# Meta rows as the fixed side of the first stage's products, and the recurrence's factors made in that stage

## The chip, the cores and the metric

The kernel runs on one core of one Trainium2 chip. The metric is the device time of one launch in microseconds (us); less is better.

## What is computed

Two transformer-like blocks run one after the other on 512 tokens of width 1024. The change touches only the first part of the first block:

```python
h = concat([zeros(112 rows), meta_tokens (16 rows), x (512 rows)])
a = rmsnorm(h, g_mix)
proj = einsum('bld,de->ble', a, w_in)                 # w_in: 1024 x 3584
sb_q, sb_k, sb_v, hg_q, hg_f, hg_i, hg_g = split(proj) # seven groups of 512 columns

o_sb = stick_breaking_attention(sb_q, sb_k, sb_v)      # 8 heads of 64
log_f = log(lb + (1 - lb) * sigmoid(hg_f))             # forget factors
k_in  = where(real, (1 - lb) * sigmoid(-hg_f), 0)      # keys
q_in  = silu(hg_q)
o_hg = hgrn2_chunked(q_in, k_in, hg_i, log_f) * silu(hg_g)   # 4 heads of 128
```

The 16 meta rows are needed only as keys and values of later rows, so their projection is made only for the groups k, v, f (`hf`) and i (`hi`). Then follow an output product, 32 experts of which each token uses two, and a second block with a convolution, a state-space branch and a feed-forward part. None of these is changed.

## The kernel before

The kernel is written instruction by instruction for each engine. TensorE (PE) multiplies, ScalarE (ACT) and VectorE (DVE) copy and combine, GpSimd (POOL) does a little elementwise work, SyncE (SP) starts the loads. Each engine has one queue in the order of its code; `wait_ge` on a semaphore orders them. The function `stage_a` holds three stages with a barrier after each (`g["clear"]`): the first stage (projections), the attention stage, and the recurrence stage.

A weight matrix is used in two halves of precision. ACT copies a loaded unit to `whi` (rounded to the product's format), DVE subtracts it from the original to get `wlo`. The normed input is kept in the same two halves, turned, as `aT_hi` and `aT_lo`. Each product is then three: low with high, high with low, and high with high.

The first stage walks over 14 units (numbered 0 to 13) of 2048 weights per partition, two for each of the groups q, k, v, hq, hf, hi, hg. For each, SP loads the unit, ACT makes `whi` (`make_hi`, line 245), DVE makes `wlo` (`make_lo`, line 320), and PE multiplies. There are two kinds of unit:

- Turned groups (q, k, hq, hf): a unit holds 256 columns in 8 pieces of depth. The weights are the fixed side (the one loaded into the array), the 512 tokens move past: lines 432, 437, 438. For k and hf the 16 meta rows move past the same weights in three products of 16 columns, lines 434 to 436.
- Plain groups (v, hi, hg): a unit holds 512 columns in 4 pieces of depth. The tokens are the fixed side in tiles of 128, the weights move past (`split_mm`, lines 48 to 50). `tiles_of` adds a fifth tile for the meta rows in v and hi; it is 128 rows wide, of which 16 are meta rows and the rest zeros.

`wused` counts units that PE has finished with. `make_hi(u)` waits for it, so that buffer u % 2 is free. ACT empties the results (`evacuate`); for k and hf it also empties the 16 meta columns of each of four column blocks.

Three things that the recurrence stage reads are made in the attention stage, between the attention's own instructions: ACT turns the sigmoids in `hfT` into forget factors (`forget`, line 621, one of four heads after each of pieces 2 to 5), DVE scales `sgn` into keys (`keys`, line 732), and POOL multiplies `q1` (line 680) and then seven levels of decays (line 686), each from neighbouring pairs of the level before.

The attention stage has 24 pieces, three for each of 8 heads. For each piece PE makes scores (lines 525 and 530), ACT takes their absolute value, exponential and logarithm (lines 599 to 603), DVE forms the sums and splits them in two halves (lines 703 to 714: the cast at 712 makes `qh`, the subtraction at 714 makes `ql`), PE sums tails over `ql` and `qh` (lines 538 to 543), ACT exponentiates (line 618). PE multiplies a head's weights with the values in `values` (line 562), once for each head, 10 products which the trace counts as 20.

## Time and profile before

| | |
|---|---|
| median of 3 runs (lowest to highest) | 2279.46 us (2278.56 to 2281.94) |
| profiled execution, its own time | 2279.0 us |
| its span, first to last instruction | 2276.8 us |
| mean granted TensorE clock | 0.940 of full speed |
| busy: PE, PE weight load, DVE, ACT, POOL | 90%, 72%, 60%, 47%, 8% |
| first stage's products, by the trace | 20.74 to 210.31 us |
| attention stage, by the trace | 210.31 to 311.66 us |

Busy shares are means over stages with different limits. The length of a matmul in the trace goes from its start to the end of its passage through the array, and the next one starts before that; how fast PE works is read from start to start. The granted clock is a share of 2.4 GHz; in a short stretch it is 1.00 (2.4 GHz), 0.50 (1.2 GHz) or a mean of the two.

### The profile page before, as it was taken

What the parts mean: (1) busy time and instruction counts of PE and PEld (TensorE: products, weight loads), DVE (VectorE), ACT (ScalarE), POOL (GpSimd) and SP (SyncE); (2) the same over time, 40 slices, a digit from 0 to 9 for tenths busy, and PEclk for the clock granted to TensorE, in tenths of its full rate; (3) what the DMA queues carried; (4) which work ended last, traced back from release to release, by engine and by line L of the source; (5) the groups of instructions that cost most, each with busy time, mean ns of one, the idle gap of its engine ahead of it and who ended that gap; (6) DMA issues with size and microseconds to landing.
All of it is one profiled execution on the core that took longest, in us unless ns stands there. A gap on an engine that the chain in (4) does not pass through costs nothing. (4 is left out here: it accounts for less than half of the span.)

```text
span 2276.8 us, 25098 instructions
## 1 busy us (share of the span) xinstructions
PE 2054.9 (90%) x10173; PEld 1636.9 (72%) x10173; DVE 1361.3 (60%) x1510; ACT 1066.6 (47%) x1252; POOL 173.3 (8%) x130
## 2 busy tenths in 40 slices
PE   7999988699999999938799999988698988999997
PEld 6887677566666666627688888877487766888786
DVE  4112775588998898842398888877533254333223
ACT  4223623388888888832334445545242233223112
POOL 1000100012222222200000000000000000000000
PEclk9999899899999999976899999999899998999999
DMA  5120004389999999851333333322222213333221
GB/s 181 61 69 1 1 1 160 114 337 403 406 402 406 400 402 395 343 178 41 94 93 93 93 93 93 93 74 56 74 78 89 92 56 85 107 95 93 92 93 56
DMA packets 201776, 346.84 MB, mean 152 GB/s; under 512 B 13587, under 2 KB 149259, under 8 KB 184251
## 3 DMA queue, kind: packets, MB, share of 16 engines
q1 hardware_dynamic: 194171, 333.42, 41.9%
q0 software_dynamic: 5120, 8.40, 1.1%
q10 hardware_dynamic: 2368, 3.39, 0.5%
q8 instruction: 82, 1.34, 0.2%
q14 instruction: 35, 0.29, 0.0%
HBM read 340.91 MB, written 12.65 MB: 155 GB/s over the span
## 5 line engine op out<-in xcount | busy, mean ns | idle before, releaser
L1492 DVE TENSOR_TENSOR wlo_e<-raw_e,whi_e 128x2048 fp32r<-128x2048 f32 x190 | 431.7, 2288 | 56.6 <-ACT whi_e L1417 56.1
L1789 DVE TENSOR_TENSOR w_lo<-w_raw,w_hi 128x2048 fp32r<-128x2048 f32 x89 | 203.8, 2289 | 322.2 <-ACT w_hi L1781 322.2
L1417 ACT CAST whi_e<-raw_e 128x2048 fp32r<-128x2048 f32 x188 | 359.2, 1912 | 74.6 <-PE pall L1568 40.7
L1781 ACT CAST w_hi<-w_raw 128x2048 fp32r<-128x2048 f32 x89 | 169.4, 1904 | 429.5 <-PE pall L50 415.1
L48 PE MATMUL pall<-hT_hi,w_lo 128*128 128x512 f32 x864 | 348.1, 403 | 23.1 <-DVE xbc L2333 10.3
L49 PE MATMUL pall<-hT_lo,w_hi 128*128 128x512 f32 x864 | 342.3, 396 | 0.0
L50 PE MATMUL pall<-hT_hi,w_hi 128*128 128x512 f32 x864 | 341.8, 396 | 0.0
L1567 PE MATMUL pall<-whi_e,xs 128*128 128x512 f32 x512 | 210.0, 410 | 4.2 <-DVE xs L1497 4.2
L48 PEld LDWEIGHTS pall<-hT_hi,w_lo 128*128 128x128 f32 x864 | 166.4, 193 | 59.7 <-DVE xbc L2333 10.5
L1568 PE MATMUL pall<-wlo_e,xs 128*64 128x512 f32 x512 | 206.3, 403 | 0.0
L50 PEld LDWEIGHTS pall<-hT_hi,w_hi 128*128 128x128 f32 x864 | 165.8, 192 | 35.5
L49 PEld LDWEIGHTS pall<-hT_lo,w_hi 128*128 128x128 f32 x864 | 166.2, 192 | 35.0 <-issue 0.5
L1567 PEld LDWEIGHTS pall<-whi_e,xs 128*128 128x128 f32 x512 | 99.4, 194 | 55.9 <-DVE xs L1497 5.4
L2318 DVE SCALAR_TENSOR_TENSOR mixed<-yT,cols,mixed 128x512 f32<-128x512 f32 x180 | 126.3, 747 | 0.0
L48 PE MATMUL pall<-w_hi,hT_lo 128*128 128x256 f32 (+1 forms) x320 | 98.9, 309 | 9.5 <-DVE hT_lo L2779 9.1
L48 PE MATMUL pall<-whi_e,hT_lo 128*64 128x512 f32 x256 | 100.6, 393 | 4.0 <-issue 2.4
L50 PE MATMUL pall<-whi_e,hT_hi 128*64 128x512 f32 x256 | 100.6, 393 | 0.0
L49 PE MATMUL pall<-wlo_e,hT_hi 128*64 128x512 f32 x256 | 100.4, 392 | 0.0
L2936 DVE TENSOR_TENSOR mixed<-mixed,pall 128x512 f32<-128x512 f32 x22 | 15.1, 688 | 139.5 <-PE pall L50 139.5
L50 PE MATMUL pall<-w_hi,hT_hi 128*128 128x256 f32 (+1 forms) x320 | 97.9, 306 | 0.0
L49 PE MATMUL pall<-w_lo,hT_hi 128*128 128x256 f32 (+1 forms) x320 | 97.8, 306 | 0.0
L971 POOL DMA_INDIRECT xg<-m_rows,row_x x32 | 81.8, 2557 | 67.4 <-PE pall L1558 36.2
(468 smaller groups left out, 3788.7 us busy)
## 6 DMA issues: line engine op xcount, KB each, us to landing
raw_e<-in_w_expert_up_dram SPq DMA_DIRECT2D x64, 1024.0 KB, 11.2
raw_e<-in_w_expert_down_dram SPq DMA_DIRECT2D x64, 1024.0 KB, 11.8
raw_e<-in_w_expert_gate_dram SPq DMA_DIRECT2D x64, 1024.0 KB, 11.7
w_raw<-in_w_in_dram SPq DMA_DIRECT2D x80, 512.0 KB, 6.2
w_raw<-in_w_gate_up_dram SPq DMA_DIRECT2D x44, 512.0 KB, 5.1
w_raw<-in_w_down_dram SPq DMA_DIRECT2D x22, 512.0 KB, 4.1
mixed<-in_w_in_dram SPq DMA_DIRECT2D x10, 1024.0 KB, 5.0
A<-acs_rows SPq DMA_DIRECT2D x8, 1024.0 KB, 4.9
```

The source lines that it names most:

```text
L48: nc.tensor.matmul(out, w_lo, m_hi, start=start, stop=False)
L49: nc.tensor.matmul(out, w_hi, m_lo, start=False, stop=False)
L50: return nc.tensor.matmul(out, w_hi, m_hi, start=False, stop=stop)
L971: pool.indirect_dma_start(xg[0:SLOTS, :], None, m_rows, bass.IndirectOffsetOnAxis(g["row_x"][0:SLOTS, b:b + 1], 0), bounds_check=T - 1, oo ...
L1417: nc.scalar.copy(whi[j], raw[j]).then_inc(sem_hi, 1)
L1492: nc.vector.tensor_tensor(wlo[j], raw[j], whi[j].bitcast(F32), ALU.subtract).then_inc(sem_lo, 1)
L1567: mm(out, x[:, kk, :], k4(whi[j])[:, k, :], start=kk == 0, stop=False, skip_group_check=True)
L1568: last = mm(out[0:SLOTS, :], x[:, kk, 0:SLOTS], k4(wlo[j])[:, k, :], start=False, stop=kk == KD - 1, skip_group_check=True)
L1781: self.nc.scalar.copy(self.hi[i][:, :], self.raw[i][:, :]).then_inc(self.s_hi, 1)
L1789: (engine or self.nc.vector).tensor_tensor(self.lo[i][:, :], self.raw[i][:, :], self.hi[i][:, :].bitcast(F32), ALU.subtract).then_inc(self ...
L2318: ins = V.scalar_tensor_tensor(mixT[:, c, :], src, col("dw_w_a", k * KD + c), mixT[:, c, :], ALU.mult, ALU.add)
L2936: V.tensor_tensor(hd, sg, banks[(2 * c + 1) % 8], ALU.mult).then_inc(s["hd"], 1)
```

## The change

The meta rows get a store of their own, `mT`, with 8 pieces of depth, each of 32 columns: 16 of the high half, 16 of the low half. The padding tile in `aT_hi` and `aT_lo` goes. In each unit of k, v, hf and hi, after the tokens' products, a new `meta_part` runs with the meta rows as the fixed side and the weights moving past: per piece of depth one product of the 32 columns with `whi`, and one of the 16 high columns with `wlo`. In k and hf the weights move in 256 columns, in v and hi in 512. After the second unit of a group ACT copies the 32 x 512 result out (`meta_sums`), and a small product with a selecting matrix `sel` adds rows 0 to 15 to rows 16 to 31 (`meta_turn`); for k and hf it also turns the result. `meta_turn` and the copy `meta_out` stand in the first unit of the next group.

`forget`, `keys`, `q1` and the decays move from the attention stage into the first. Some buffers share memory with others to make room, and a clearing of the meta buffer at the start is gone.

```diff
@@ tiles
             def tiles_of(what):
-                return [0, 1, 2, 3] if what == "hg" else [0, 1, 2, 3, 4]
+                return [0, 1, 2, 3]
@@ gpsimd, first stage (the same lines are taken out of the attention stage)
+                pool.wait_ge(s["mask"], 1)
+                pool.wait_ge(s["f"], HG_HEADS)
+                nc.gpsimd.tensor_tensor(q1[:, :, :], hqT[:, :, :], hfT[:, :, META:TM], ALU.mult).then_inc(s["q1"], 1)
+                for i, w in enumerate(WIDE):
+                    if i >= 1:
+                        pool.wait_ge(s["dec"], i)
+                    of = decay[w // 2][:, :, 1:1 + T // 16] if w == 32 else decay[w // 2][:, :, :]
+                    pairs = of.rearrange("p e (n two) -> p e n two", two=2)
+                    nc.gpsimd.tensor_tensor(decay[w][:, :, :], pairs[:, :, :, 0], pairs[:, :, :, 1], ALU.mult).then_inc(s["dec"], 1)
@@ scalar, first stage
+                def meta_sums(m, u):
+                    act.wait_ge(s["wused"], u + 1)
+                    if m >= 1:
+                        act.wait_ge(s["mt"], m)
+                    nc.scalar.copy(msb[:, :], MB[0:2 * META, :]).then_inc(s["ms"], 1)
+
+                def meta_out(what):
+                    act.wait_ge(s["mt"], META_OF[what] + 1)
...
+                    if half == 0 and u >= 1 and units[u - 1][1] in META_OF:
+                        if u + 2 < len(units):
+                            make_hi(u + 2)
+                        meta_out(units[u - 1][1])
+                        if units[u - 1][1] == "hf":
+                            act.wait_ge(s["evac"], o)
+                            act.wait_ge(s["mev"], META_OF["hf"] + 1)
+                            for e in range(HG_HEADS):
+                                forget(e)
+                        continue
+                    if half and what in META_OF:
+                        meta_sums(META_OF[what], u)
@@ vector, first stage
                 for u in range(2, len(units)):
                     make_lo(u)
+                dve.wait_ge(s["mev"], META_OF["hf"] + 1)
+                dve.wait_ge(s["evac"], 20)
+                dve.wait_ge(s["lb"], 2)
+                for e in range(HG_HEADS):
+                    keys(e)
@@ tensor, first stage
+                def meta_part(what, half, wh, wl):
+                    if half == 0 and META_OF[what] >= 1:
+                        pe.wait_ge(s["ms"], META_OF[what])
+                    wide = wh.shape[-1]
+                    c = slice(half * wide, half * wide + wide) if wide == 256 else slice(0, wide)
+                    for k in range(wh.shape[1]):
+                        kk = k if wide == 256 else 4 * half + k
+                        st, sp_ = (k == 0, k == KD - 1) if wide == 256 else (kk == 0, kk == KD - 1)
+                        nc.tensor.matmul(MB[0:2 * META, c], mT[:, kk, :], wh[:, k, :], start=st, stop=False, skip_group_check=True)
+                        last = nc.tensor.matmul(MB[0:META, c], mT[:, kk, 0:META], wl[:, k, :], start=False, stop=sp_,
+                                                skip_group_check=True)
+                    return last
+
+                def meta_turn(what):
+                    m = META_OF[what]
+                    pe.wait_ge(s["ms"], m + 1)
+                    pe.wait_ge(s["sel"], 1)
+                    if m >= 1:
+                        pe.wait_ge(s["mev"], m)
+                    if what in ("k", "hf"):
+                        for e in range(4):
+                            last = nc.tensor.matmul(MT[:, e * META:e * META + META], msb[:, e * P:e * P + P], sel[:, :], start=True,
+                                                    stop=True)
+                    else:
+                        last = nc.tensor.matmul(MT[0:META, :], sel[:, :], msb[:, :], start=True, stop=True)
+                    last.then_inc(s["mt"], 1)
...
                                 nc.tensor.matmul(b[:, :], w_l, a_hi, start=st, stop=False)
-                                if is_meta_turned(what):
-                                    nc.tensor.matmul(bm[:, 0:META], w_l, m_hi, start=st, stop=False)
-                                    nc.tensor.matmul(bm[:, 0:META], w_h, m_lo, start=False, stop=False)
-                                    nc.tensor.matmul(bm[:, 0:META], w_h, m_hi, start=False, stop=sp_)
                                 nc.tensor.matmul(b[:, :], w_h, a_lo, start=False, stop=False)
...
+                    if half == 0 and u >= 1 and units[u - 1][1] in META_OF:
+                        meta_turn(units[u - 1][1])
+                    if what in META_OF:
+                        meta_part(what, half, wh, wl).then_inc(s["wused"], 1)
@@ attention stage
-                    if 2 <= n < 2 + HG_HEADS:
-                        forget(n - 2)
...
-                    if 6 <= n < 6 + HG_HEADS:
-                        keys(n - 6)
```

How the instructions move is shown at three places. First PE's queue in a unit of k, over one piece of depth. Before, with the three products of 16 columns (the last size in a row is that of the result):

```order
L432 MATMUL pall<-aT_hi,wlo_a 128x512
L434 MATMUL pall<-aT_hi,wlo_a 128x16
L435 MATMUL pall<-aT_lo,whi_a 128x16
L436 MATMUL pall<-aT_hi,whi_a 128x16
L437 MATMUL pall<-aT_lo,whi_a 128x512
L438 MATMUL pall<-aT_hi,whi_a 128x512
```

After, at the end of the same unit, where the tokens' products are followed by those of the meta rows (`mT_a` is `mT`), eight pairs in all:

```order
L533 MATMUL pall<-aT_hi,wlo_a 128x512
L534 MATMUL pall<-aT_lo,whi_a 128x512
L535 MATMUL pall<-aT_hi,whi_a 128x512
L490 MATMUL pall<-whi_a,mT_a 32x256
L491 MATMUL pall<-wlo_a,mT_a 16x256
L490 MATMUL pall<-whi_a,mT_a 32x256
L491 MATMUL pall<-wlo_a,mT_a 16x256
```

The narrow products no longer stand between wide ones. Second, PE's queue in the first unit of v, after the last tokens' products; the first row is `meta_turn` for k, the rest are the meta rows of v:

```order
L503 MATMUL pall<-sel,meta_rows 128x16 x4
L490 MATMUL pall<-whi_a,mT_a 32x512
L491 MATMUL pall<-wlo_a,mT_a 16x512
L490 MATMUL pall<-whi_a,mT_a 32x512
L491 MATMUL pall<-wlo_a,mT_a 16x512
```

They stand where the fifth tile of lines 48 to 50 stood. Third, POOL's queue. Before, `q1` (called `q` here) and the decays come last in the attention stage:

```order
L677 AFFINE_SELECT own_rows<-own_rows 128x8
L680 TENSOR_TENSOR q<-hqT,hfT 128x2048
L686 TENSOR_TENSOR decay<-hfT 128x1056
L686 TENSOR_TENSOR decay<-decay 128x528
L686 TENSOR_TENSOR decay<-decay 128x264
```

After, they follow POOL's only large instruction of the first stage, ahead of the barrier:

```order
L229 TENSOR_TENSOR wlo_a<-mixed,whi_a 128x2048
L232 TENSOR_TENSOR q<-hqT,hfT 128x2048
L238 TENSOR_TENSOR decay<-hfT 128x1056
L238 TENSOR_TENSOR decay_rest<-decay 128x528
L238 TENSOR_TENSOR decay_rest<-decay_rest 128x264
```

On ACT the four `forget` instructions now stand in unit 10, between the cast for unit 12 and the copies of unit 11's results:

```order
L266 CAST whi_a<-mixed 128x2048
L334 ACTIVATE hfT<-pall 128x4x16
L335 ACTIVATE sgn<-pall 128x4x16
L341 ACTIVATE hfT<-hfT,lb,omlb 128x528 x4
L317 COPY hv_nat<-pall 128x512 x4
L326 COPY meta_rows<-pall 32x512
L266 CAST whi_a<-mixed 128x2048
```

In the attention stage they stood singly behind pieces 2 to 5.

## Rows read from the trace of the kernel before

**Rows 1.** Windows over two stages: length, busy time and instructions by engine, clock, DMA.

```profile
20.74:210.31 189.57, 189.53 (x924) 159.19 (x924) 36.00 (x34) 50.38 (x71) 0.00 (x0) 0.99 0.19 62
210.31:311.66 101.35, 90.78 (x381) 61.09 (x381) 70.65 (x135) 61.76 (x118) 13.01 (x21) 0.85 0.00 1
```

**Rows 2.** Timeline of PE in the first stage: start, length, line, operation.

```profile
45.36 0.39 PE L432 MATMUL pall<-aT_hi,wlo_a 128*128 128x512 f32 x1
...
46.04 0.39 PE L432 MATMUL pall<-aT_hi,wlo_a 128*128 128x512 f32 x1
...
62.55 0.40 PE L432 MATMUL pall<-aT_hi,wlo_a 128*128 128x512 f32 x1
```

**Rows 3.** Timeline of PE in the attention stage.

```profile
225.29 1.12 PE L580 MATMUL pall<-v_nat,pick_m 16*128 16x512 f32 x2
...
232.75 2.39 PE L562 MATMUL pall<-v_nat,ww 128*128 128x64 f32 x20
...
241.33 2.40 PE L562 MATMUL pall<-v_nat,ww 128*128 128x64 f32 x20
...
253.95 4.47 PE L562 MATMUL pall<-v_nat,ww 128*128 128x64 f32 x20
...
268.77 2.39 PE L562 MATMUL pall<-v_nat,ww 128*128 128x64 f32 x20
...
277.36 2.39 PE L562 MATMUL pall<-v_nat,ww 128*128 128x64 f32 x20
```

**Rows 4.** Timeline of POOL in the attention stage.

```profile
242.03 4.54 POOL L680 TENSOR_TENSOR q<-hqT,hfT 128x2048 f32<-128x2048 f32 x1 [27.36 <-ACT hfT L621]
...
248.73 3.83 POOL L686 TENSOR_TENSOR decay<-decay 128x528 f32<-128x528 f32 x6
```

**Rows 5.** Timeline of DVE in the attention stage.

```profile
233.01 0.43 DVE L712 CAST qh<-qq 128x512 fp32r<-128x512 f32 x1
...
242.10 4.75 DVE L712 CAST qh<-qq 128x512 fp32r<-128x512 f32 x1
246.89 2.31 DVE L714 TENSOR_TENSOR ql<-qq,qh 128x512 fp32r<-128x512 f32 x1
```

**Rows 6.** Windows of 3.4 us in the attention stage.

```profile
247.60:251.00 3.40, 1.74 (x7) 1.31 (x7) 3.23 (x4) 1.64 (x3) 3.17 (x4) 0.92 0.00 0
251.00:254.40 3.40, 3.40 (x12) 2.74 (x11) 3.26 (x9) 2.11 (x5) 1.33 (x4) 0.50 0.03 7
...
268.00:271.40 3.40, 3.40 (x28) 3.10 (x27) 2.09 (x5) 1.92 (x4) 0.00 (x0) 1.00 0.00 0
```

**Rows 7.** Timeline of ACT in the first stage, late units.

```profile
177.67 0.59 ACT L294 COPY hv_nat<-pall 128x512 f32<-128x512 f32 x1 [0.76 <-PE pall L50]
...
188.55 0.59 ACT L294 COPY hv_nat<-pall 128x512 f32<-128x512 f32 x1 [2.13 <-PE pall L50]
189.03 1.91 ACT L245 CAST whi_a<-mixed 128x2048 fp32r<-128x2048 f32 x1
...
202.15 0.60 ACT L296 ACTIVATE hg_nat<-pall 128x512 f32<-128x512 f32 x1 [9.91 <-PE pall L50]
```

**Rows 8.** Timeline of PE far behind, products of 256 columns.

```profile
1299.77 0.28 PE L49 MATMUL pall<-w_lo,hT_hi 128*128 128x256 f32 x1
...
1303.97 0.28 PE L48 MATMUL pall<-w_hi,hT_lo 128*128 128x256 f32 x1
```

**Rows 9.** Timeline of PE, where products of 128 and 64 output columns meet.

```profile
802.70 0.40 PE L1568 MATMUL pall<-wlo_e,xs 128*64 128x512 f32 x1
802.98 0.41 PE L48 MATMUL pall<-whi_e,hT_lo 128*64 128x512 f32 x1
803.24 0.39 PE L49 MATMUL pall<-wlo_e,hT_hi 128*64 128x512 f32 x1
```

**Rows 10.** Timeline of DVE in the first stage, late.

```profile
190.97 2.29 DVE L320 TENSOR_TENSOR wlo_a<-mixed,whi_a 128x2048 fp32r<-128x2048 f32 x1 [11.74 <-ACT whi_a L245]
```

**Rows 11.** Timeline of ACT in the attention stage, one step of forget().

```profile
241.13 0.81 ACT L621 ACTIVATE hfT<-hfT,lb,omlb 128x528 f32<-128x528 f32 x1
```

More of the change, by code:

```diff
@@ L93, in stage_a @@
         ident_r = sb("ident_r", [P, P], F32R)
+        q1 = sb("q1", [P, HG_HEADS, T])
+        WIDE = (2, 4, 8, 16, 32, 64, 128)
+        sizes = [TM // w if w <= META else T // w for w in WIDE]
+        decay2 = sb("decay2", [P, HG_HEADS, sizes[0]])
+        decay_rest = sb("decay_rest", [P, HG_HEADS * sum(sizes[1:])])
+        decay, at = {1: hfT, 2: decay2}, 0
+        for w, n in zip(WIDE[1:], sizes[1:]):
+            decay[w] = decay_rest[:, at:at + HG_HEADS * n].rearrange("p (e n) -> p e n", e=HG_HEADS)
+            at += HG_HEADS * n
         s = {n: sem("a_" + n) for n in (
-            "x meta vec gbc ident ones eps hm0 ssq rt rs xn tr hi lo vtr cols lbd lb whi wlo wused out evac "
-            "it xor xf up ge mask never wlo0".split())}
+            "x meta vec gbc ident ones eps ssq rt rs xn tr hi lo vtr cols lbd lb whi wlo wused out evac "
+            "it xor xf up ge mask never wlo0 sel ms mt mev f kx q1 dec".split())}
         s_x = [sem(f"a_x{i}") for i in range(NT)]
@@ L143, in stage_a @@
                     outs.append((what, e))
-            def is_meta_turned(what):
-                return what in ("k", "hf")
+            META_OF = {"k": 0, "v": 1, "hf": 2, "hi": 3}
+            MB, MT = banks[6], banks[7]
             def turn_bank(j):
@@ L245, in make_hi, with upper_meta @@
                     nc.scalar.copy(whi[u % 2][:, :], raw[u % 3]).then_inc(s["whi"], 1)
+                def upper_meta():
+                    act.wait_ge(s["tr"], 2 * NT + 1)
+                    nc.scalar.copy(mT[:, :, 0:META], banks[6][:, 0:KD * META].rearrange("p (k t) -> p k t", k=KD)).then_inc(s["hi"], 1)
                 def upper(j):
@@ L282, in evacuate @@
                     elif what == "k":
-                        nc.scalar.copy(kT[:, e, META:TM], b[:, :])
-                        last = nc.scalar.copy(kT[:, e, 0:META], banks[6 + e % 2][:, 0:META])
+                        last = nc.scalar.copy(kT[:, e, META:TM], b[:, :])
                     elif what == "hf":
                         for dst, sign in ((hfT, 1.0), (sgn, -1.0)):
-                            nc.scalar.activation(dst[:, e, META:TM], b[:, :], ACT.Sigmoid, scale=sign)
-                            last = nc.scalar.activation(dst[:, e, 0:META], banks[6 + e % 2][:, 0:META], ACT.Sigmoid, scale=sign)
+                            last = nc.scalar.activation(dst[:, e, META:TM], b[:, :], ACT.Sigmoid, scale=sign)
                     elif what == "v":
@@ L297, in evacuate, with forget @@
                     last.then_inc(s["evac"], 1)
+                def meta_sums(m, u):
[5 more added lines that the diff above has]
+                    act.wait_ge(s["mt"], META_OF[what] + 1)
+                    by_e = MT[:, 0:4 * META].rearrange("p (e t) -> p e t", e=4)
+                    if what == "k":
+                        last = nc.scalar.copy(kT[:, :, 0:META], by_e)
+                    elif what == "hf":
+                        nc.scalar.activation(hfT[:, :, 0:META], by_e, ACT.Sigmoid)
+                        last = nc.scalar.activation(sgn[:, :, 0:META], by_e, ACT.Sigmoid, scale=-1.0)
+                    else:
+                        last = nc.scalar.copy((v_nat if what == "v" else hv_nat)[0:META, NT, :], MT[0:META, :])
+                    last.then_inc(s["mev"], 1)
+                def forget(e):
+                    nc.scalar.activation(hfT[:, e, :], hfT[:, e, :], ACT.Identity, bias=lb[:, e:e + 1],
+                                         scale=omlb[:, e:e + 1]).then_inc(s["f"], 1)
                 o = 0
@@ L352, in _ @@
                 make_lo(1)
-                lower(4)
+                lower_meta()
+                nc.vector.tensor_tensor(sel[:, :], ident[0:2 * META, 0:META], ident[0:2 * META, META:2 * META],
+                                        ALU.add).then_inc(s["sel"], 1)
                 dve.wait_ge(s["vtr"], 1)
@@ L402, in turn, with turn_meta @@
                         last.then_inc(s["tr"], 1)
+                def turn_meta():
+                    pe.wait_ge(s["xn"], NT + 1)
+                    for k in range(KD):
+                        last = nc.tensor.transpose(banks[6][:, k * META:k * META + META], xn[NT % 2][0:META, k * P:k * P + P],
+                                                   ident[0:META, 0:META])
+                    last.then_inc(s["tr"], 1)
+                def meta_part(what, half, wh, wl):
[20 more added lines that the diff above has]
+                                                    stop=True)
+                    else:
+                        last = nc.tensor.matmul(MT[0:META, :], sel[:, :], msb[:, :], start=True, stop=True)
+                    last.then_inc(s["mt"], 1)
                 for j in range(NT):
@@ L409, in _ @@
                     if u == 1:
-                        turn(NT)
+                        turn_meta()
                         vectors()
@@ L452, in _ @@
                             if j == tiles_of(what)[-1]:
-                                last.then_inc(s["wused"], 1)
+                                if what not in META_OF:
+                                    last.then_inc(s["wused"], 1)
                             elif half:
```

69 lines of the change are left out of this document (28 added, 41 removed).

## The prediction

> **What bounds the kernel now.** I read the windows by stage first, then PE's timeline in the first stage, then PE, POOL and DVE side by side in the attention stage.
>
> In the first stage PE is the bound: in 189.57 us of products it is busy 189.53 us at a granted clock of 0.99, DVE works 36.0 us and ACT 50.4 us [rows 1]. What PE no longer does there comes off the time, one for one, as long as the halves `whi` and `wlo` come in time. The reader is to see that a product of 512 columns costs 0.227 us from start to start (0.68 us for the three of a piece of depth) [rows 2].
>
> In the attention stage the pace is read from one `values` to the next, once for each head [rows 3]. From 232.75 to 241.33 and from 268.77 to 277.36 us a head takes 8.58 and 8.59 us. In between it takes 12.62 us and then 14.82 us. The first of these slow heads falls together with POOL's chain, 242.03 to 252.56 us [rows 4]. In it DVE's cast to `qh`, elsewhere 0.43 us, takes 4.75 us and the subtraction behind it 2.31 us [rows 5]. PE runs dry (1.74 us busy in a window of 3.40) [rows 6], and right behind that hole its clock falls from 0.92 to 0.50 (1.2 GHz) and is back at 1.00 (2.4 GHz) in the window that begins at 268.00 [rows 6]. The second slow head runs wholly at the lower level. So POOL's chain costs time twice: by DVE's stop, and by the clock that falls after it.
>
> The cast began 0.07 us after POOL's product of 4.54 us and ended 0.28 us after it. The Trainium skill (SBUF — State Buffer, Who interferes with whom) says that VectorE and GpSimd share one pair of ports, that casts and subtractions with both inputs in SBUF need it, and that the loser waits for the whole instruction. By that rule the trace agrees: a full stop, not a slower cast.
>
> **The change part by part.** The sum is made against the profiled execution, 2279.0 us, which is 0.5 us under the median of the runs.
>
> *Taken away in the first stage.* Groups k and hf have 64 places (2 groups, 4 column blocks, 8 pieces of depth) with three products of 16 columns. A place with them takes (62.55 - 46.04) / 16 = 1.032 us, one without takes 0.68 us (45.36 to 46.04) [rows 2]. That is 0.352 us each, 22.5 us in all: narrow products cost far more than their columns, since each stands behind a weight load. The fifth tile of v and hi: ACT's copies follow one another in 2.72 us, four steps from 177.67 to 188.55 [rows 7]; one tile of 12 products in each of 4 units is 10.9 us. Together 33.4 us.
>
> *Added in the first stage.* Groups k and hf: 4 units with 16 products of 256 columns. The trace has a long row of such products, with a wide fixed side: 35 steps from 1299.77 to 1303.97, 0.120 us each [rows 8]; 64 of them are 7.7 us. Groups v and hi: 4 units with 8 products of 512 columns, 32 x 0.227 = 7.3 us. The fixed side is narrower than any in these rows, and its load should hide behind the product before it as the wide one does. The selecting products: for v and hi one full-precision product of 512 columns each, like the 1.12 us row with 16 rows of depth [rows 3], 2.2 us; for k and hf four each of 16 columns, 8 passes at 2.39 / 20 = 0.12 us [rows 3], 1.9 us. A change between products of different width: where 128 and 64 output columns meet, the two steps are 0.28 and 0.26 us instead of 0.227 [rows 9], 0.08 us together; the eight `meta_part` have 16 such edges, 1.3 us. Together 20.4 us.
>
> The bounds of this part: 256 columns could cost as much as 512 if the load showed, 0.227 us, 7 us more; the selecting products could run at the lower clock, twice 4.1 us, 4 us more. Below 0.120 us I know nothing that would take the 256 columns.
>
> The Trainium skill (TensorEngine Tiling (Array Packing), Key Properties) says that a change of tiling mode drains TensorE. A drained step would show the whole passage: 0.39 us instead of 0.227, 0.16 us more. The edge shows 0.08 us for two steps, so I take the smaller [rows 9]; a drain at each of the 96 narrow products is a rival below.
>
> *The first stage's other engines, costed at nothing.* The last unit is the tightest: its cast starts at 189.03, its subtraction runs 190.97 to 193.26 [rows 7, 10], and PE needs it when unit 13 begins, one tile before the copy at 202.15, so at 199.4. The slack is 6.2 us. `forget` (0.81 us each) [rows 11], behind the cast of 1.91 us for unit 12, ends some 5.5 us after the end of unit 10. POOL's chain of 10.5 us then runs to 16 us after it. Unit 11 takes 10.9 + 1.8 = 12.7 us, the cast for unit 13 ends about 15.8 us after the end of unit 10, and the subtraction meets only the last small levels of the chain. Even the full 4.5 us of the largest product in its way would leave 1.7 us. Queued behind the longer ACT list are the copies of hi's tiles, whose banks PE wants only a unit later. `meta_turn` waits for a copy made a whole unit of tokens earlier. SP's loads wait for the subtraction and have two units of lead. If this cover were gone, a late `wlo` would cost PE what exceeds 6.2 us.
>
> First stage: -33.4 + 20.4 = -13.0 us.
>
> *The attention stage.* Neither `forget` nor `keys` costs time there now: heads with a `forget` between (232.75 to 241.33) and heads without take the same 8.59 us [rows 3]. What goes is POOL's chain. If the two slow heads take the pace of the others, the gain is (268.77 - 241.33) - 2 x 8.59 = 10.3 us. Its bounds: 4.0 us if only the stop goes (12.62 - 8.59) and the clock falls all the same, and upwards, since the clock of the whole stage is 0.85 [rows 1], which is 30 us at the lower level of which 17 lie behind the hole [rows 6]: 13 us at the lower level lie elsewhere, worth 6.5 us if they went too. I have no reason for that and take 10.3.
>
> Sum: 2279.0 - 13.0 - 10.3 = 2255.7, against the median 2256.2. I say **2256 us**, 1.0% faster.
>
> **The rivals.**
>
> *Only the stop goes, the clock falls anyway* (chance 0.10): the attention stage works PE in short bursts, and the clock level that PE keeps there may depend on more than this hole; its first microseconds, where POOL is not at fault, are part of the 13 us above. Against it: the heads at 8.59 us ran at 1.00 without a hole. Gain 13.0 + 4.0, time 2262 us.
>
> *The narrow products don't stream* (0.08): the load of a narrow fixed side shows, or the array drains. With 256 columns at 0.227 us it is 2263 us; with 0.16 us more at each of 96 products, 15.4 in place of the 1.3, it is 2270 us. Against it: 128 and 64 output columns in turn cost little [rows 9]. The drain is what the Trainium skill (TensorEngine Tiling (Array Packing), Key Properties) would make of it if 32 and 16 columns are two modes.
>
> *A slower kernel* (0.03): PE's clock falls in the first stage. Eight units now end in about 2 us of narrow products. A fall as long as the one that is over at 268.00 us [rows 6], some 17 us, costs 8.5 us. The gain is 23.3 us, and 4.6 us more would have to be lost before the result reads as slower: four such falls decide it, and after all eight the time would be 2324 us. Against it: the clock was 0.99 in this stage with 192 products of 16 columns among the others [rows 1].
>
> *No change* (0.03): the halves come late by POOL's chain or ACT's longer list and PE waits in two or three units, eating 20 us. The slack of 6.2 us per unit speaks against it.
>
> **How the numbers follow.** The forecast has 0.76, the rivals 0.10, 0.08, 0.03 and 0.03. The forecast's own bounds are 2256 - 6.5 = 2249 and 2256 + 4 = 2260. The range takes in the first two rivals nearly whole, 2247 to 2266; outside it remain the drain, the no-change case and the slower one. A difference of 0.2% (4.6 us) is about what a measurement of this kernel can tell from none. Faster by more than that holds the forecast and both first rivals, 0.94; within it 0.03; slower 0.03.
>
> **What would show each step.** In the changed trace the products L490 and L491 follow each other in 0.12 us at 256 columns and 0.23 us at 512. The stage's products end about 13 us earlier, near 197 us, at a clock of 0.99. The cast for unit 13 is not late, and PE shows no idle time ahead of a unit. POOL's chain stands between the units 11 and 12. In the attention stage all eight cycles of `values` take 8.6 us, the cast to `qh` is never over 0.5 us, the clock stays at 1.00 after its first rise, and the stage is about 91 us long. The prediction is wrong if the clock falls at a new place, if steps of the narrow products are nearer 0.2 us, or if a later stage's pace changes, in which I see nothing that the change touches.

## The result, and the profile after

| | before | after |
|---|---|---|
| first comparison, median of 7 runs (lowest to highest) | 2280.45 us (2276.82 to 2285.96) | 2264.67 us (2260.77 to 2272.14) |
| ratio, 95% interval | | 0.9943 (0.9927 to 0.9960) |
| all runs of the study, mean (number of runs) | 2278.7 us (77) | 2260.9 us (20) |
| profiled execution, its own time and span | | 2261.14 us, 2259.4 us |
| its granted clock; busy PE, DVE, ACT, POOL | | 0.943; 90%, 60%, 47%, 8% |

The change makes the kernel faster. 0.9943 of 2279.46 us is 2266.5 us, 10 us above the forecast of 2256 and half a microsecond above the top of its range. Two later comparisons of the same two kernels gave ratios of 0.9926 (0.9900 to 0.9953) and 0.9912 (0.9886 to 0.9939). Over all runs the gain is 17.7 us, plus or minus 2.6 (each mean's spread is 5.1 to 5.3 us a run), where 23.3 us were forecast.

Windows over the two stages of the changed kernel, columns as in [rows 1]:

```profile
20.61:197.97 177.36, 177.36 (x799) 139.35 (x800) 36.66 (x38) 53.66 (x68) 9.40 (x8) 0.99 0.20 66
197.97:289.71 91.74, 83.50 (x383) 56.03 (x382) 62.80 (x131) 59.38 (x114) 2.96 (x13) 0.93 0.00 1
```

PE's last product of the first stage starts at 197.97 us; before it started at 209.88. PE is busy throughout, at the same clock of 0.99. The attention stage is 91.7 us long. PE's timeline in the first stage:

```profile
45.11 0.39 PE L533 MATMUL pall<-aT_hi,wlo_a 128*128 128x512 f32 x1
...
45.81 0.39 PE L533 MATMUL pall<-aT_hi,wlo_a 128*128 128x512 f32 x1
...
57.01 0.28 PE L490 MATMUL pall<-whi_a,mT_a 128*32 128x256 f32 x1
57.12 0.28 PE L491 MATMUL pall<-wlo_a,mT_a 128*16 128x256 f32 x1
57.24 0.28 PE L490 MATMUL pall<-whi_a,mT_a 128*32 128x256 f32 x1
...
58.83 0.39 PE L533 MATMUL pall<-aT_hi,wlo_a 128*128 128x512 f32 x1
...
82.93 1.06 PE L503 MATMUL pall<-sel,meta_rows 32*128 32x16 f32 x8
83.92 0.42 PE L490 MATMUL pall<-whi_a,mT_a 128*32 128x512 f32 x1
...
85.80 0.40 PE L48 MATMUL pall<-whi_a,aT_lo 128*128 128x512 f32 x1
```

The narrow products stream: 16 of 256 columns take 58.83 - 57.01 = 1.82 us, 0.114 each, and 8 of 512 take 1.88 us (83.92 to 85.80). `meta_turn` takes 0.99 us (82.93 to 83.92). But the reader should look at the first two rows: a piece of depth, three products of 512 columns that the change did not touch, takes 0.70 us here and took 0.68 before [rows 2].

The engines beside PE, late in that stage (POOL, then ACT, then DVE):

```profile
167.83 4.64 POOL L232 TENSOR_TENSOR q<-hqT,hfT 128x2048 f32<-128x2048 f32 x1 [147.37 <-ACT hfT L341]
...
175.60 2.10 POOL L238 TENSOR_TENSOR decay_rest<-decay_rest 128x264 f32<-128x264 f32 x5
```

```profile
164.68 3.00 ACT L341 ACTIVATE hfT<-hfT,lb,omlb 128x528 f32<-128x528 f32 x4
...
176.21 1.90 ACT L266 CAST whi_a<-mixed 128x2048 fp32r<-128x2048 f32 x1
```

```profile
178.14 2.29 DVE L375 TENSOR_TENSOR wlo_a<-mixed,whi_a 128x2048 fp32r<-128x2048 f32 x1 [11.46 <-ACT whi_a L266]
180.35 1.70 DVE L404 TENSOR_SCALAR sgn<-sgn,omlb 128x528 f32<-128x528 f32 x4
```

POOL's chain ends at 177.7 us, in the gap between two of DVE's subtractions, and the last `wlo` is ready at 180.4, 6.7 us before PE begins its unit at 187.1. In the attention stage, PE's timeline at the values:

```profile
220.85 2.39 PE L658 MATMUL pall<-v_nat,ww 128*128 128x64 f32 x20
229.44 2.39 PE L658 MATMUL pall<-v_nat,ww 128*128 128x64 f32 x20
238.03 2.39 PE L658 MATMUL pall<-v_nat,ww 128*128 128x64 f32 x20
246.61 2.39 PE L658 MATMUL pall<-v_nat,ww 128*128 128x64 f32 x20
```

A head is the time from one `values` to the next. Both slow heads [rows 3] have gone: 8.58 to 8.60 us each (only the last two are shorter, 8.04 and 5.05 us, as before). When POOL opens the recurrence stage, at 289.71 us instead of 311.89, the lead over the kernel before is 22.2 us, close to the forecast. When PE starts the first product of the stage behind it, at 348.67 us instead of 366.36, the lead is 17.7 us: from POOL's opening to there it took 58.96 us, and before 54.47. PE's timeline in the recurrence stage, then windows where the attention stage opens and behind the recurrence's hole, in this execution and in another one of the same kernel (e, below):

```profile
325.43 0.60 PE L892 MATMUL pall<-ident,sgn 128*16 128x128 f32 x4
327.59 2.58 PE L898 MATMUL pall<-ident,sgn 128*128 128x128 f32 x12 [1.56 <-DVE q L932]
```

```profile
200.00:212.00 12.00, 12.00 (x24) 5.98 (x23) 9.77 (x25) 7.99 (x17) 2.55 (x13) 0.57 0.00 1
326.00:338.00 12.00, 10.44 (x48) 9.88 (x48) 7.23 (x20) 2.34 (x4) 0.00 (x0) 0.58 0.01 1
```

```profile
200.00:212.00 12.00, 11.78 (x34) 5.67 (x35) 9.89 (x26) 10.45 (x21) 2.94 (x13) 1.00 0.01 1
326.00:338.00 12.00, 10.11 (x88) 9.76 (x87) 7.83 (x28) 6.34 (x35) 0.00 (x0) 1.00 0.00 1
```

PE waits 1.56 us for DVE's `q`, and behind the hole its clock is at the lower level: 48 products in 12 us where the other execution, at 1.00, does 88. The same wait stands in the kernel before, at 349.48 us, with no fall behind it. So one execution of each kernel does not say what the change does, and the study turned to two questions: which clock falls belong to the kernel, and why untouched products became longer. On the first, the expectations below call it "phase" if a fall behind the same hole comes in one execution of a program and not in the next, and "systematic" if it belongs to the program.

### The profile page after: what moved, and what is told of

Read it like the earlier page. It is cut to its first block and busy times, and to the rows that moved or that the text cites. A ratio compares the mean times of both kernels' runs of the same rounds, so it can differ in the third digit from the quotient of the medians.

```text
span 2259.4 us, 24849 instructions
## 1 busy us (share of the span) xinstructions
PE 2039.1 (90%) x10049; PEld 1615.0 (71%) x10049; DVE 1353.3 (60%) x1509; ACT 1069.4 (47%) x1246; POOL 169.8 (8%) x130
## 5 line engine op out<-in xcount | busy, mean ns | idle before, releaser
L48 PE MATMUL pall<-hT_hi,w_lo 128*128 128x512 f32 x864 | 347.2, 402 | 23.9 <-DVE xbc L2410 10.3
L1645 PEld LDWEIGHTS pall<-wlo_e,xs 128*64 128x64 f32 x512 | 70.7, 138 | 21.5
```

Source lines behind the costliest of these rows:

```text
L48: nc.tensor.matmul(out, w_lo, m_hi, start=start, stop=False)
L1645: last = mm(out[0:SLOTS, :], x[:, kk, 0:SLOTS], k4(wlo[j])[:, k, :], start=False, stop=kk == KD - 1, skip_group_check=True)
```

## The experiments

**a and b: each kernel once more, unaltered.**

> The changed kernel once more, unaltered, for a second trace. Theory (phase): the first stage's products end near 198.4 us again and the eight cycles of the attention stage take 8.6 us again, so the first two stages repeat to 0.3 us. The 1.6 us hole of PE late in the recurrence stage is there again, but whether the clock falls to 0.50 behind it changes from run to run: the recurrence stage, from POOL's clearing of the store to the end of its last product, takes 52.4 us with the fall and some 48 without. Rival (systematic): the fall is part of the changed kernel, it comes again at the same place and lasts 10 us again.

> The kernel before once more, unaltered, for a second trace. Theory (phase): POOL's chain again stops DVE's cast for some 4.7 us and a head takes about 12.6 us; the clock's fall behind it may be there or not, so the second slow head takes 8.6 to 15 us. In the recurrence stage the clock may now fall behind the hole where it did not before. Rival (systematic): the same two slow heads (12.6 and 14.8 us) and no fall in the recurrence stage.

Measured: 2266.59 and 2270.88 us, one run each. The changed kernel again has no slow head. This time the clock stays at 1.00 when the attention stage opens, and from the first stage's last product to the first `values` it takes 18.10 us instead of 22.88; nothing falls behind the recurrence's hole either. The kernel before, PE's timeline:

```profile
235.92 2.41 PE L562 MATMUL pall<-v_nat,ww 128*128 128x64 f32 x20
247.02 2.39 PE L562 MATMUL pall<-v_nat,ww 128*128 128x64 f32 x20
255.60 2.39 PE L562 MATMUL pall<-v_nat,ww 128*128 128x64 f32 x20
```

POOL's stop is there (a head of 11.10 us), the fall behind it is not: the next head takes 8.58 us, not 14.82. The stop alone costs 11.10 - 8.59 = 2.5 us. The 4.0 us that the forecast had for it (12.62 - 8.59) held some of the fall: in that head PE was at 0.50 from 251.00 us on [rows 6].

**c: the meta rows' part alone.** The factors, keys and decays stay in the attention stage (against the changed kernel):

```diff
 gpsimd, first stage
-                pool.wait_ge(s["f"], HG_HEADS)
-                nc.gpsimd.tensor_tensor(q1[:, :, :], hqT[:, :, :], hfT[:, :, META:TM], ALU.mult).then_inc(s["q1"], 1)
...
 scalar, attention stage
+                    if 2 <= n < 2 + HG_HEADS:
+                        forget(n - 2)
```

> Only the meta rows' part: forget, keys, q1 and the decays stay in the attention stage. Both theories: the first stage's products end 11 to 12 us earlier than before, at 198 to 199 us; POOL's chain is back in the attention stage with one head at 12.6 us. Phase theory: time 9 to 14 us under before, ratio about 0.995. Rival (the give-back belongs to the fifth tile or the new products): under 6 us.

Measured in 12 runs: ratio 0.9960 (0.9942 to 0.9979), mean 9.3 us under the 23 runs of the kernel before beside it. PE's timeline:

```profile
229.21 2.41 PE L632 MATMUL pall<-v_nat,ww 128*128 128x64 f32 x20
241.70 4.47 PE L632 MATMUL pall<-v_nat,ww 128*128 128x64 f32 x20
256.67 2.39 PE L632 MATMUL pall<-v_nat,ww 128*128 128x64 f32 x20
```

Stop and fall are both there (heads of 12.49 and 14.97 us). The first stage is shorter by as much as in the changed kernel.

**d: the factors' part alone**, with the padding tile kept, 64 rows wide (against the kernel before):

```diff
-            aT_hi = sb("aT_hi", [P, KD, T + P], F32R, ctx=tmp)
+            aT_hi = sb("aT_hi", [P, KD, T + 64], F32R, ctx=tmp)
...
+                    if what == "hi" and half == 0:
+                        act.wait_ge(s["evac"], o)
+                        for e in range(HG_HEADS):
+                            forget(e)
```

> Only the factors' part: forget, keys, q1 and the decays in the first stage, the meta rows' products as before (the padding tile is 64 rows wide in place of 128, to make room; its products have as many columns). Both theories: the first stage's products end as before, near 210 us; all cycles of the attention stage take 8.6 us. Phase theory: 4 to 10 us under before, the 4 being the stop alone and 10 the stop and the fall, ratio 0.9965 with the mean of the two. Rival (POOL's chain in the first stage delays the subtraction for unit 13 and PE waits): under 2 us or slower.

Measured in 12 runs: ratio 0.9971 (0.9953 to 0.9988), mean 5.4 us under the kernel before. No head is slow. The two parts add up to 14.7 us, which is the whole within their errors (by the intervals, some 4 us each).

**e and j: the changed kernel again, on two chips.**

> The changed kernel unaltered, timed again beside the others. Phase theory: ratio 0.992 to 0.996 as in the first measurement, and a third trace in which the first stage's products end between 197.9 and 199.3 us, all heads take 8.6 us, and the falls of the clock at the entry of the attention stage (about 200 to 212 us) and behind the hole of the recurrence stage are there or not, independent of each other. Rival (systematic): both falls again.

> The changed kernel unaltered, on the same chip. Theory (the same program's clock falls differ from one execution to the next, the stages' own work does not): last start of the first stage at 198 to 199, eight heads of 8.59 us, entry either 18.1 or 22.9 us, ratio to the kernel before 0.992 to 0.995. Rival (the entry's fall is fixed by the program and the earlier difference was of the chip): the entry is the same as in the run beside it on this chip.

Measured: ratios 0.9926 and 0.9912, as above. Both profiles show 18.10 us from the first stage's last product to the first `values`, and no fall behind the recurrence's hole. The run beside j (i) shows no fall where the attention stage opens either, so these alone would fit the rival, a fall that goes by the chip. But e and g (below) ran on one chip and open the attention stage with the same code, and take 18.10 and 22.89 us: the fall differs from execution to execution.

**f: the changed kernel with POOL's chain put back where it was**, on a spare buffer, nothing reading it:

```diff
+                pool.wait_ge(s["w"], 6)
+                gp.tensor_tensor(scr[:, :, 0:T], hqT[:, :, :], hfT[:, :, META:TM], ALU.mult).then_inc(s["scr"], 1)
+                for i, n in enumerate((264, 132, 66, 33, 16, 8, 4)):
+                    pool.wait_ge(s["scr"], i + 1)
...
```

> The changed kernel, with a chain of the same lengths put back on POOL alone in the attention stage, after piece 5: it reads the same stores and writes a scratch tile that nobody reads. forget and keys stay in the first stage. If POOL's chain is what made the slow heads: one head at 11 to 12.6 us again, DVE's cast at 4.7 us, the next head 8.6 or up to 15 us by the clock, and 3 to 9 us over the changed kernel. If the slow heads came from forget or keys between the attention's instructions: all heads at 8.6 us, no difference.

Measured in 12 runs: ratio 0.9971 (0.9944 to 0.9999), mean 8.6 us above the changed kernel's 20 runs (11.2 above the six of e beside it). POOL, DVE and PE at the place:

```profile
229.08 4.55 POOL L771 TENSOR_TENSOR scr<-hqT,hfT 128x2048 f32<-128x2048 f32 x1 [26.07 <-ACT ww L715]
```

```profile
229.27 4.77 DVE L797 TENSOR_TENSOR qq<-qq 128x384 f32<-128x384 f32 x1
234.08 2.05 DVE L802 CAST qh<-qq 128x512 fp32r<-128x512 f32 x1
```

```profile
229.61 2.39 PE L659 MATMUL pall<-v_nat,ww 128*128 128x64 f32 x20
240.78 2.39 PE L659 MATMUL pall<-v_nat,ww 128*128 128x64 f32 x20
249.36 2.39 PE L659 MATMUL pall<-v_nat,ww 128*128 128x64 f32 x20
```

DVE's sum of 384 elements takes 4.77 us, until POOL's product of 4.55 us is done: another instruction than in [rows 5], the same stop. The head takes 11.17 us, the next 8.59. The slow head was POOL's doing; `forget` and `keys`, which this kernel keeps in the first stage, have no part in it.

**g and h: more work for PE at two holes**, in the changed kernel and in the one before: 25 filler products at the end of the attention stage and 6 in the recurrence's hole.

```diff
+                for _ in range(25):
+                    mm(pall[:, 4, :], ident_r[:, :], keep_r[:, 0:4, :].rearrange("p b t -> p (b t)"), start=True, stop=True)
```

> The changed kernel with products that nobody reads in two holes of PE: 25 of 512 columns behind the last products of the attention stage (5.7 us in a hole of 6.8) and 6 ahead of the turning of the keys in the recurrence stage (1.4 us in a hole of 1.6). Phase theory: the clock stays at 1.00 from the attention stage through the recurrence stage; the recurrence stage takes the short time in every run, 2 us less at its start and 4.7 us less in those runs in which the clock fell; 2 to 6 us under the changed kernel. Rival (the clock has no part in it): no gain, or the filler's own time is lost.

> The kernel before with the same fillers. Phase theory: 2 to 6 us under the kernel before; the difference to the changed kernel with fillers is what the change is worth with these two places quiet: 12 us for the meta rows, 3 to 4 for the stop of DVE, and the fall behind it in the runs that have it, 15 to 20 us. Rival: the give-back is elsewhere, and the difference stays 13 to 15 us.

Measured: g 0.9923 (0.9901 to 0.9945, 6 runs), not told apart from the changed kernel, so the 2 to 6 us expected did not show; h 0.9973 (0.9955 to 0.9991, 12 runs), mean 5.8 us under the kernel before, as expected. With the fillers in both, the change is worth 12.4 us, plus or minus some 4.5. That is under the 15 to 20 us expected and nearest to the rival's 13 to 15; no run says why. Windows over the first filler's place, in g and in the changed kernel:

```profile
282.00:298.00 16.00, 14.88 (x103) 13.18 (x101) 13.21 (x27) 3.84 (x8) 1.80 (x1) 1.00 0.00 1
```

```profile
282.00:298.00 16.00, 9.20 (x60) 8.53 (x59) 11.55 (x23) 3.80 (x8) 1.81 (x1) 0.79 0.00 1
```

The fall there goes (1.00 against 0.79), and the recurrence stage takes 52.7 us in both kernels against 54.2 to 55.2 in most others. In g another fall then stands at 340 to 348 us (clock 0.58). h also shows POOL's stop followed by a fall, and b without one, from holes that are alike. First the windows of b, then those of h:

```profile
240.00:244.00 4.00, 1.60 (x6) 0.53 (x5) 3.86 (x3) 1.48 (x4) 3.92 (x3) 1.00 0.00 0
244.00:260.00 16.00, 16.00 (x88) 12.03 (x88) 15.24 (x32) 11.23 (x22) 2.78 (x6) 1.00 0.01 2
```

```profile
240.00:244.00 4.00, 1.61 (x6) 0.53 (x4) 3.92 (x2) 1.49 (x4) 3.92 (x3) 0.86 0.00 0
244.00:260.00 16.00, 15.99 (x46) 11.40 (x46) 12.16 (x26) 6.26 (x13) 2.92 (x6) 0.50 0.01 2
```

PE works 1.60 and 1.61 of 4 us; then it does 88 products at 1.00 in one execution and 46 at 0.50 in the other.

**i: fillers where the attention stage opens**, two behind each of the first three score steps of the changed kernel.

> The changed kernel with two filler products of 512 columns behind each of the first three score steps of the attention stage, 6 in all, 1.4 us by the 0.23 us step. Theory (the fall at the stage's entry comes from TensorE being lightly used there, and is there in one execution and not in the next): with the fillers the entry shows no clock of half, the time from the last start of the first stage to the first `values` is 18.1 + 1.4 = 19.5 us or less instead of 22.9, all heads that POOL doesn't stop take 8.6 us, and against the changed kernel the mean falls by 0.6 x 4.8 - 1.4 = 1.5 us, at the edge of what can be measured. Rival (the fall is not moved by six products): the entry still shows 22.9 + 1.4 = 24.3 us in some profile, and the time is 1.4 us above the changed kernel's.

Measured in 6 runs: 0.9921 (0.9889 to 0.9952), mean 1.6 us above j's, no difference that can be told. The profile shows 19.47 us at a clock of 1.00, as the theory had it; but j without fillers had no fall either. Whether the fillers keep it away stays open. This profile has a short fall behind the recurrence's hole instead (0.74 and 0.84 in two windows of 4 us from 322.12 us on).

**k and l: where things lie in memory.** The first stage is shorter by less than the narrow products explain, since the untouched ones became longer. In the changed kernel the rows of `aT_hi` stand 2048 bytes apart (2560 before, 2304 in d). And by the program's addresses `whi` lies 49152 bytes behind `aT_hi` before and 45056 in d, both whole multiples of 2048; in the changed kernel it is 44096, which is 21 x 2048 + 1088. k changes the row distance, l adds a gap of 960 bytes ahead of the halves:

```diff
 k
-            aT_hi = sb("aT_hi", [P, KD, T], F32R, ctx=tmp)
-            aT_lo = sb("aT_lo", [P, KD, T], F32R, ctx=tmp)
+            aT_hi = sb("aT_hi", [P, KD, T + 16], F32R, ctx=tmp)
+            aT_lo = sb("aT_lo", [P, KD, T + 16], F32R, ctx=tmp)
 l
+            gap = sb("gap_a", [P, 240], ctx=tmp)
```

> The first stage lost 11.9 us where the sum said 13.0, and its traces give the reason in small change: a product of 512 columns of plain tokens takes 0.2267 us from start to start in the kernel before (and in the kernel with the factors alone), but 0.2289 us in the plain groups and 0.2334 us in the turned ones with the meta rows' own store, 672 products in all, 2 to 4 us. What differs is where things lie: without the padding tile the rows of aT_hi and aT_lo stand 2048 bytes apart instead of 2560 (2304 with the factors alone), and the halves of the weights have another offset to them. Here the changed kernel gets 16 unused columns behind each row of aT_hi and aT_lo, 2112 bytes apart. Theory A (the distance of 2048 bytes): steps of 0.2267 us in q, hq and hg, last start of the first stage 2 to 3 us earlier, near 195.5. Rival B (the halves' offset): steps stay at 0.2289 and 0.2334 us, last start at 198 to 199.5. Rival C (neither; something the meta products themselves do): the same as B here.

> The changed kernel with 960 unused bytes ahead of the halves of the weights, so that whi and wlo have the same offset modulo 2048 bytes as aT_hi and aT_lo, as in the kernel before; the rows of aT stay 2048 bytes apart. Theory A (the distance): steps stay at 0.2289 and 0.2334 us, last start at 198 to 199.5. Rival B (the offset): steps of 0.2267 us in q, hq and hg, last start near 195.5. Rival C (neither): as A here, and as B in the other kernel.

Measured, 6 runs each: k 0.9935 (0.9916 to 0.9954), l 0.9904 (0.9886 to 0.9921). **m and n** then put 64 bytes of gap into the changed kernel and into the one before.

> The changed kernel with 64 unused bytes ahead of the halves of the weights. In the changed kernel whi stands 64 bytes past a multiple of 1024 from aT_hi (44096 = 43 x 1024 + 64), in the kernel before, in the one with the factors alone and in the one with 960 bytes of gap it stands a whole multiple of 1024 away; here it is 128 past one. Theory A (what counts is whether the two lie alike within 128 bytes): steps of 0.2267 us, last start of the first stage near 195.8 to 197.0. Rival B (they must lie alike within 256 bytes or more): steps stay above 0.2285 us, last start at 198 to 199.5.

> The kernel before, unaltered but for 64 unused bytes ahead of the halves of the weights, so that they stand 64 bytes past a multiple of 2048 from aT_hi instead of on one. Theory (the offset alone sets the step of a product, whatever the meta rows do): the steps of q, hq, hi and hg rise from 0.2267 to 0.2289 us in the plain groups and 0.2334 us in the turned ones, and the first stage ends 2 to 3 us later, last start at 211.5 to 213. Rival (it takes the changed kernel's layout or its products as well): steps stay at 0.2267 us, last start at 209 to 210.

Measured once each: 2266.36 and 2287.78 us. What counts is in the traces. `vectors` is a few small transposes in the first unit; nothing but products stands behind it. Windows from the first product behind `vectors` to the last start of the first stage, one row for each kernel, in the order before, n, changed kernel, k, m, l:

```profile
35.04:209.88 174.84, 174.84 (x866) 147.43 (x865) 32.71 (x32) 48.52 (x68) 0.00 (x0) 1.00 0.17 55
```

```profile
34.50:210.98 176.48, 176.48 (x867) 147.54 (x865) 32.72 (x32) 48.53 (x68) 0.00 (x0) 1.00 0.16 54
```

```profile
34.52:197.97 163.45, 163.45 (x742) 128.28 (x741) 33.43 (x36) 52.13 (x66) 9.40 (x8) 1.00 0.18 58
```

```profile
35.18:198.89 163.71, 163.71 (x742) 128.37 (x741) 33.42 (x36) 52.07 (x66) 9.38 (x8) 1.00 0.17 58
```

```profile
35.42:199.60 164.18, 164.18 (x743) 128.67 (x741) 33.42 (x36) 52.09 (x66) 9.39 (x8) 1.00 0.18 58
```

```profile
35.02:195.82 160.80, 160.80 (x743) 128.29 (x741) 33.41 (x36) 52.10 (x66) 9.38 (x8) 1.00 0.18 59
```

PE is busy from end to end, all at 1.00, and repeats of one kernel agree to 0.01 us (174.84 in before, b and h), so such a row resolves what no timing here does. The gap of 960 bytes alone takes the changed kernel from 163.45 to 160.80 us, 2.65 us. The step of a 512-column product is 0.2289 us in the plain groups and 0.2334 in the turned ones in the changed kernel, 0.2267 in both in l. PE's timeline in hq over two pieces of depth (six steps), first in the changed kernel, then in l:

```profile
102.15 0.39 PE L533 MATMUL pall<-aT_hi,wlo_a 128*128 128x512 f32 x1
...
103.55 0.39 PE L533 MATMUL pall<-aT_hi,wlo_a 128*128 128x512 f32 x1
```

```profile
102.18 0.39 PE L534 MATMUL pall<-aT_hi,wlo_a 128*128 128x512 f32 x1
...
103.54 0.39 PE L534 MATMUL pall<-aT_hi,wlo_a 128*128 128x512 f32 x1
```

k has 0.2317 nearly everywhere, m 0.232 to 0.233. n, the kernel before with its halves moved by 64 bytes, has 0.2289 in v, hi, hg and 0.2334 in q and hq, exactly the changed kernel's steps. In k and hf, where the narrow products of before still stand, the same gap makes one of the wide steps shorter (from 0.233 to 0.228 us) and another longer, and a place costs 1.033 us with it and without. So the whole costs n 1.64 us, less than the 2 to 3 expected.

So the step goes with the offset between the buffers of the fixed and the moving side (B). It is 0.2267 us in the three kernels in which that is a whole multiple of 2048 bytes (before, d, l), at three row distances, and longer in the four in which it is not. The halves' own place in memory doesn't decide it: `whi` begins 544 bytes past a multiple of 2048 before and 736 past one in d and l, with the same step. But the offset alone does not give the size. The wider rows of k also moved the halves, to 22 x 2048 + 64 bytes behind `aT_hi`; that is n's offset, and yet its steps are not n's. So the row distance, or where `aT_lo` lies, has a part that no run here separates, and k by itself doesn't clear the row distance. l does: its rows stay 2048 bytes apart and the step is the short one. m's theory A fell too.

## Why the prediction was off

**First stage: -13.0 us forecast, -11.4 measured** (174.84 - 163.45). By parts, from PE's timeline: the 256-column products take 7.3 us (7.7 forecast), the 512-column ones 7.5 (7.3), the four turns 3.9 (4.1). Added were thus 18.7 us where the forecast had 20.4. The edges cost next to nothing (1.3 us forecast): the 16 products between two wide ones take 1.82 us, 0.114 each, so "a drain at each of the 96 narrow products" did not happen and "the narrow products don't stream" is refuted; where the Trainium skill (TensorEngine Tiling (Array Packing), Key Properties) speaks of a drain, fixed sides of 32, 16 and 128 columns follow one another here without one: the step from the last wide product to the first narrow one is 57.01 - 56.78 = 0.23 us. With the halves at a whole multiple of 2048 bytes (l) the gain is 14.0 us, a microsecond more than forecast. What failed in this stage is a step that the sum took without saying so: it left the 672 token products at 0.227 us, a term of nothing. The smaller buffers moved the halves to another offset, and that took 2.65 us back.

**The cover: right.** DVE's last `wlo` takes 2.29 us and no unit waits; the slack is 6.7 us (6.2 before the change, by the forecast's reading). POOL's chain stands where the order said.

**Attention stage: -10.3 us forecast.** The cause was right: the stop is POOL's (f), and it goes with the chain (no head above 8.7 us in all ten traces without the chain there). "Only the stop goes, the clock falls anyway" is refuted at this place by the same ten. The size is the other step that failed: "if the two slow heads take the pace of the others, the gain is (268.77 - 241.33) - 2 x 8.59". That prices two things as if both came in every run. In the six traces with the chain in the attention stage the stop is there six times, worth 2.5 us, and the fall behind it four times (12.5 and 15.0, 13.6 and 14.9, 13.6 and 14.8 us beside the 12.62 and 14.82 of [rows 3]; b and f without). The mean of the six excesses over 17.18 us is 8.0 us. Six traces fix that mean to some 1.7 us (standard error), so the 2.3 us between it and 10.3 rest on the count of four in six; f's timing, 8.6 us for the chain put back, agrees with it but cannot tell the two apart. The 10.3 us themselves were there in the two profiled executions.

**"A later stage's pace changes, in which I see nothing"** named the risk, not the way: the fall behind the recurrence's hole, 4.5 us, stood in one profiled execution: 58.96 us for the stretch from POOL's opening of the recurrence stage to the next stage's first product, which takes 54.2 to 55.2 us in 12 of the others (52.7 with fillers in g and h, 56.3 in i). It doesn't come with the change each time, since a, e and j ran the same program without it. Whether the change makes it likelier is not shown: in the five traces with the old meta products it is never there, in the eleven with the new ones once clearly and once briefly (i).

So by the traces the gain is 11.4 + 8.0 = 19.4 us where 23.3 were forecast, and 17.7 plus or minus 2.6 were measured. These two terms are 3.9 us of the 10 by which the first comparison missed the forecast. The 1.7 us from 19.4 to 17.7 are within the errors. The rest, 4.7 us, is chance: the first comparison's ratio is a gain of 13.0 us, plus or minus 3.8, and the two later ones give 16.9 and 20.1.

**A cross-check by the clock.** Every run lists its mean granted clock. Over 70 runs of the kernel before, 0.001 of it goes with 1.8 us (two of them: 2270.65 us at 0.946, 2287.04 at 0.938). A straight line through each kernel's runs, read at 0.943, leaves what is not clock:

| at clock 0.943 | us | to before | by the traces, without falls |
|---|---|---|---|
| before | 2276.3 | | |
| changed | 2262.6 | -13.7 | -11.4 - 2.5 = -13.9 |
| c, meta rows alone | 2265.6 | -10.7 | -11.4 |
| d, factors alone | 2274.2 | -2.1 | -2.5 |
| f, chain put back | 2264.9 | -11.4 | -11.4 |
| l, gap of 960 bytes | 2257.8 | -18.5 | -14.0 - 2.5 = -16.5 |

The scatter about a line is 2.6 us a run, the standard error of a line 0.4 to 1.3 us. f's line is steeper than the others (2.5 us per 0.001); with the slope of before it would stand at 2266.3. By the same reading g and h, with the fillers, are 14.9 us apart (2261.2 and 2276.2). l lies 2 us lower than its traces say. The remainder of the gain, 17.7 - 13.7 = 4.0 us, goes with the clock: the changed kernel's mean is 0.0021 higher, which at 1.8 us per 0.001 is 3.8. It is a correlation over runs; only the profiled ones say where a fall stood.

**The best version** is l: 2257.57 us mean of 6 runs, 21.8 us under the kernel before beside it, against 17.7 for the change as it stands. By timing alone the two are hardly apart; the traces' 2.65 us, at full clock with PE never idle, are what says that it is faster.

## What to carry to other kernels

Split a stall's price into the wait itself, which came in every trace here, and the clock fall behind it, which did not; a single profile can't tell how often, so weigh the fall by repeated profiles or put it into the range. When a change resizes or moves buffers, compare the steps of instructions that it did not touch: here the offset between the fixed and the moving side's buffers was worth 2.65 us, a fifth of the first stage's gain, and 960 unused bytes bought it back (160.80 instead of 163.45 us). A part where one engine is busy from end to end at one clock can be read to 0.01 us, where timing this kernel needs many runs to see 3 us.

## What the runs showed of the hardware

- The step of a 512-column product depends on how the buffers of fixed and moving side lie to each other: 0.2267 us with a whole multiple of 2048 bytes between them, 0.2289 or 0.2334 with 64 bytes more (n) or 1088 (changed kernel), 0.2317 with 64 bytes more and wider rows (k), 0.232 to 0.233 with 1152 (m). Where the two reads meet wasn't tried.
- Fixed sides of 32 and 16 columns cost no more than wide ones: 0.114 us a step at 256 moving columns, where the wide fixed side took 0.120 [rows 8].
- PE's clock falls behind the same hole in one execution and not in the next: behind POOL's stop in 4 of 6 traces, behind the recurrence's hole clearly in 1 of 16 and briefly in another (i), and where the attention stage opens (last product to first `values` 22.9 us instead of 18.1) in 9 of 16, with one more at 21.3 us.
- 25 filler products where PE would idle kept the clock at 1.00 there (0.79 without). With them and six more at the next hole the changed kernel's time stayed the same within what 6 runs can tell, and the kernel before became 5.8 us shorter (0.9955 to 0.9991).
- POOL's product of 4.55 us stopped the DVE instruction that began just behind it in all six traces that have it in the attention stage: casts of 0.43 us took 4.75 to 4.77 us, in f a sum of 384 elements 4.77.
